# Six gate products cut in halves and put between the steps of the delta rule's inverses

## What is computed

```python
def first_block(x, ...):
    for l in range(DEPTH):                                  # two layers
        h = rmsnorm(x, norm_mix_g[l])
        proj = h @ w_in[l]
        (qa, ka, va, qd, kd, vd, beta_logit, decay_logit, z, gate_logit) = jnp.split(proj, offsets, axis=-1)
        ...
        y_attn = grid_attention(qa, ka, va) @ w_o_attn[l]
        qkv = jax.nn.silu(centred_depthwise_conv(jnp.concatenate([qd, kd, vd], axis=-1), dn_conv_w[l]))
        ...
        o = bidir_gated_deltanet(qd, kd, vd, beta, g)       # chunks of 64 tokens, 8 heads, both directions
        o = rmsnorm(o, dn_out_norm_g[l]) * jax.nn.silu(z)
        y_dn = o.reshape(b, s, DN_V) @ w_o_dn[l]
        gates = jax.nn.sigmoid(gate_logit).reshape(b, s, N_BRANCH, D_MODEL)
        mixed = gates[:, :, 0] * y_attn + gates[:, :, 1] * y_dn
        x = x + mixed @ w_out[l]
        ...                                                 # a feed-forward part
def second_block(x, mem, ...):
    for l in range(DEPTH):                                  # two layers
        h = _rmsnorm(x, norm_g[l])
        z = h @ w_in[l]
        ...
```

## Time and profile before

| | us |
|---|---|
| median of 3 runs | 3692.01 (3689.04 to 3694.11) |
| the profiled execution | 3687.55 |
| its span, first to last instruction | 3685.6 |
| TensorE busy in the span | 3377.2 |
| VectorE busy | 1894.9 |
| ScalarE busy | 1555.4 |
| GpSimd busy | 218.6 |

### The profile page before, as it was taken

One profiled execution on the slowest core, in us unless ns is written; L12 is line 12 of the kernel. 1 busy time (PEld: TensorE's weight loads), 2 busy tenths in 40 slices (PEclk: granted clock), 3 DMA queues, 4 the chain that ended last, 5 costly groups with the idle time before them and its releaser, 6 DMA issues. The chain is left out here.

```text
span 3685.6 us, 61547 instructions
## 1 busy us (share of the span) xinstructions
PE 3377.2 (92%) x26780; PEld 2658.0 (72%) x26780; DVE 1894.9 (51%) x2834; ACT 1555.4 (42%) x2612; POOL 218.6 (6%) x204
## 2 busy tenths in 40 slices
PE   7887899999998887999999988989999979989999
PEld 4576777778875676877788865767777757767787
DVE  5565554575566555554756554452434544534343
ACT  6533223433347433233433355546443455463432
POOL 0032330000000131300000000000000000000000
PEclk9897999999999988999999999999999989999999
DMA  3000003332231000023233231211122312111222
GB/s 136 29 14 19 25 14 124 102 97 92 92 116 46 13 19 25 23 75 101 87 97 103 84 114 52 76 38 60 55 83 71 114 32 78 52 55 61 66 69 94
DMA packets 74925, 249.09 MB, mean 68 GB/s; under 512 B 9249, under 2 KB 10913, under 8 KB 73377
## 3 DMA queue, kind: packets, MB, share of 16 engines
q1 hardware_dynamic: 74656, 245.16, 20.4%
HBM read 237.82 MB, written 6.29 MB: 66 GB/s over the span
## 5 line engine op out<-in xcount | busy, mean ns | idle before, releaser
L470 PE MATMUL psum<-s_h,s_w 128*128 128x512 f32 (+1 forms) x6864 | 1672.7, 400 | 50.9 <-DVE s_h L1782 20.4
L470 PEld LDWEIGHTS psum<-s_h,s_w 128*128 128x128 f32 (+1 forms) x6864 | 1294.1, 191 | 360.7 <-issue 43.3
L1782 DVE TENSOR_TENSOR s_w<-s_stage,s_w 128x1024 fp32r<-128x1024 f32 (+2 forms) x468 | 522.7, 1119 | 493.8 <-ACT s_w L1169 491.5
L1169 ACT ACTIVATE s_w<-s_stage 128x1024 fp32r<-128x1024 f32 (+2 forms) x468 | 450.9, 966 | 304.4 <-PE psum L470 279.4
L1169 ACT ACTIVATE s_tmp<-psum 128x512 f32<-128x512 f32 (+2 forms) x192 | 110.0, 573 | 364.1 <-PE psum L470 356.3
L470 PE MATMUL psum<-s_ffa,s_w 128*128 128x512 f32 x1056 | 249.0, 396 | 3.8 <-DVE s_ffa L1782 3.8
L470 PEld LDWEIGHTS psum<-s_ffa,s_w 128*128 128x128 f32 x1056 | 197.5, 187 | 54.3 <-DVE s_ffa L1782 6.4
L470 PE MATMUL psum<-s_oR,s_w 128*128 128x512 f32 (+1 forms) x960 | 223.2, 383 | 11.5 <-DVE s_w L1782 5.7
L1169 ACT ACT_TABLE_LOAD x169 | 216.8, 1283 | 7.8 <-DMA s_x<-xT 4.8
L470 PEld LDWEIGHTS psum<-s_oR,s_w 128*128 128x128 f32 x960 | 169.0, 192 | 47.9 <-DVE s_w L1782 6.7
L1169 ACT ACTIVATE s_E<-psum,s_nm 128x256 f32<-128x256 f32 (+3 forms) x224 | 114.5, 516 | 195.4 <-DVE s_nm L1864 195.4
(11 more groups left out here) (252 smaller groups left out, 3491.9 us busy)
## 6 DMA issues: line engine op xcount, KB each, us to landing
s_stage<-w SPq DMA_DIRECT2D x192, 512.0 KB, 3.3
s_stage<-wup SPq DMA_DIRECT2D x88, 512.0 KB, 3.3
s_stage<-wo SPq DMA_DIRECT2D x32, 512.0 KB, 3.3
s_stage<-wdn SPq DMA_DIRECT2D x32, 512.0 KB, 3.5
s_stage<-wdn SPq DMA_DIRECT2D x16, 384.0 KB, 3.1
spill<-s_x SPq DMA_DIRECT2D x2, 2048.0 KB, 8.3
s_stage<-woa SPq DMA_DIRECT2D x16, 256.0 KB, 2.7
s_x<-spill SPq DMA_DIRECT2D x2, 2048.0 KB, 8.1
```

The costliest lines, as they stand in the source:

```text
L470: return self.e.matmul(out, left, right, start=first, stop=last, skip_group_check=True)
L1169: return self.e.activation(out, src, func, **kw)
L1782: return self.e.tensor_tensor(out, a, b, op)
```

## The change

Six of the eight gate products of branch d leave branch d. A new generator `plug` makes them in halves of 12 matmuls. `plugged` lets it take one half at the listed turns: two at the start of the delta rule's scalars, five in `units(0)`, one in `chain(l, 0)`, four in `units(1)`. ACT takes the tanh at once into a new tile `early2`. Meanwhile the other fill products there make their weights only one product ahead instead of two.

The triangle mask on the queries' part is no longer a multiplication by POOL: DVE takes the minimum with a constant that is 0 inside the triangle and very negative outside it, so that the exponential is zero there; DVE then writes the query products straight to M2, and the 16 multiplications of POOL fall away. In the second block `normal` runs all eight columns at once behind q product 0. The size of the DMA scratch goes from 4096 to 2048.

```diff
-    def mixed(self, l, attention, scalars, begun, project, gates):
+    def mixed(self, l, attention, scalars, begun, project, gates, plug):
...
-        beside(abreast(scalars, begun, delayed(project(0, (1,)), 2)), fill, 1, 1)
-        beside(units(0), fill, 5, 6)
-        beside(self.chain(l, 0), fill, 5, 6)
+        beside(plugged(abreast(scalars, begun, delayed(project(0, (1,)), 2)), plug, (0, 1)), fill, 1, 1)
+        beside(plugged(units(0), plug, (4, 5, 21, 22, 33)), fill, 5, 6)
+        beside(plugged(self.chain(l, 0), plug, (0,)), fill, 5, 6)
...
-        beside(units(1), fill, 5, 4)
+        beside(plugged(units(1), plug, (4, 5, 21, 22)), fill, 5, 4)
...
+def plugged(steps, plug, turns):
+    for n, _ in enumerate(steps):
+        if n in turns:
+            next(plug, None)
+        yield
...
-            if name == "d" or c >= 4:
+            if c >= (PLUGS if name == "d" else 4):
...
+    def plug(self, l, hi, lo, ht):
+        for c in range(PLUGS):
+            yield from self.lin_steps((l, "d", "g", c), self.d["w1"][l, 30 + c], 8, hi, lo, ht, 4, ("act_mix", l, "d", c))
...
-                self.ahead(key)
+                self.ahead(key, 1)
...
+    def plug(self, l):
+        for c in range(PLUGS):
+            key = (l, "d", "g", c)
+            self.ahead(key, 1)
+            yield
+            g = self.k.tmp[l, "d", c, "gate"] = self.m.early2[:, c, :]
+            self.w.wait_ge(*self.prod(key))
+            self.f(g, self.bank(key), ACT.Tanh, scale=0.5).then_inc(*self.up("act_mix", l, "d", c))
+            yield
...
-        uppers = self.uppers(("two", l), hi, 4)
+        uppers = self.uppers(("two", l), hi, 8)
...
-        self.e.tensor_scalar(X, Pm, 0.0, None, ALU.min).then_inc(*self.up("vec_unit", key, "a1"))
+        self.tt(v8(X), v8(Pm), B(m.cstm[:, M_BU + r, None, :], 1, 8), ALU.min).then_inc(*self.up("vec_unit", key, "a1"))
...
-            self.tt(X[:, s], X[:, s], self.bank((both, "kq", e))[:, 256:512], ALU.mult).then_inc(*self.up("vec_unit", key, "q", e))
+            self.tt(m.M2[:, r, jp, s], X[:, s], self.bank((both, "kq", e))[:, 256:512], ALU.mult).then_inc(*self.up("vec_unit", key, "q", e))
...
-        self.w.wait_ge(*self.at("pool_unit", key, "M2"))
+        self.w.wait_ge(*self.at("vec_unit", key, "q", 1))
+        self.w.wait_ge(*self.at("pool_unit", key, "X1"))
...
-                next(normal, None)
-                next(normal, None)
+                for _ in normal:
+                    pass
...
-        self.w.wait_ge(*self.at("vec_unit", key, "q", 1))
-        self.tt(v8(m.M2[:, r, jp, :]), v8(X), over(M_TU + r), ALU.mult).then_inc(*self.up("pool_unit", key, "M2"))
```

More of the change, by code:

```diff
@@ L21 @@
 LAG = 3
+PLUGS = 6
 ORDER_A = (4, 0, 5, 1, 6, 2, 7, 3)
@@ L36 @@
 M_ID = 14
-M_N = 15
+M_BU = 15
+M_N = 17
 def constants():
@@ L60, in constants @@
     zm[:, M_ID] = row == c64
+    zm[:, M_BU] = np.where(row <= c64, 0.0, NEG)
+    zm[:, M_BU + 1] = np.where(row >= c64, 0.0, NEG)
     for k in range(6):
@@ L364, in __init__ @@
                 self.oat, self.o = sm("oat", [128, 4, T]), sm("dno", [128, 4, T])
+                self.early2 = sm("early", [128, PLUGS, T])
                 self.zs = [sm("qkv", [128, 2, 2, T]), self.x[:, 4:8, :].rearrange("p (a b) t -> p a b t", a=2)]
@@ L494, in lin, with lin_steps @@
         last.then_inc(*self.up("prod", self.used - 1))
-    def lin_steps(self, key, src, kt, hi, lo, made, per):
+    def lin_steps(self, key, src, kt, hi, lo, made, per, free=None):
         whi, wlo = self.weights(key, src, kt)
@@ L506, in lin_steps @@
                 last.then_inc(*self.up("prod", n))
+                if free is not None:
+                    self.give(key, free)
             if k % per == per - 1:
@@ L728, in layer1 @@
         self.mixed(l, lambda: self.attention(A, f), scalars, begun, lambda g, js: self.project(l, g, js, hi, lo, ht),
-                   lambda: itertools.chain(self.gates(l, hi, lo, ht), self.early(l, hi, lo, ht)))
+                   lambda: itertools.chain(self.gates(l, hi, lo, ht), self.early(l, hi, lo, ht)),
+                   self.plug(l, hi, lo, ht))
         def branch(name, c, gate, w, made, a):
-            if name == "d" or c >= 4:
+            if c >= (PLUGS if name == "d" else 4):
                 self.lin((l, name, "g", c), wt[l, gate + c], 8, hi, lo, ht)
@@ L917, in chain @@
         for r in range(2):
-            self.after([("act_unit", (l, g, 1, r), "w"), ("vec_unit", (l, g, 1, r), "w"), ("pool_unit", (l, g, 1, r), "M2")])
+            self.after([("act_unit", (l, g, 1, r), "w"), ("vec_unit", (l, g, 1, r), "w"), ("vec_unit", (l, g, 1, r), "q", 1)])
         heads = [(jp, e) for jp in range(2) for e in range(2)]
@@ L1377, in layer1 @@
         self.mixed(l, lambda: self.attention(("A", l), grid_attn(m, l)), scalars, begun, lambda g, js: self.project(l, g, js),
-                   lambda: itertools.chain(self.gates(l), self.early(l)))
+                   lambda: itertools.chain(self.gates(l), self.early(l)), self.plug(l))
         self.w.wait_ge(*self.at("vec_chain", (l, 1), "o", 7, 1))
@@ L1962, in layer1 @@
         for c in range(8):
-            self.ahead((l, "d", "g", c))
+            if c >= PLUGS:
+                self.ahead((l, "d", "g", c))
             self.ahead((l, "d", c))
@@ L2171, in gates, with plug @@
             yield
+    def plug(self, l):
+        for c in range(PLUGS):
+            self.ahead((l, "d", "g", c), 1)
+            yield
+            yield
     def early(self, l):
         for c in range(4):
-            self.ahead((l, "a", "g", c))
+            self.ahead((l, "a", "g", c), 1)
             for _ in range(5):
@@ L2691 @@
     from concourse.bass_utils import run_bass_kernel_spmd as _run
-    nc = _bacc.Bacc("TRN2", target_bir_lowering=False, num_devices=1, dynamic_dma_scratch_size=4096)
+    nc = _bacc.Bacc("TRN2", target_bir_lowering=False, num_devices=1, dynamic_dma_scratch_size=2048)
     arrays = arrange(inputs)
```

## The result

| | before | after |
|---|---|---|
| median of 4 runs, us | 3693.06 (3689.04 to 3698.52) | 3643.89 (3643.32 to 3646.85) |
| profiled execution, us | 3687.55 | 3644.41 |
| its span, us | 3685.6 | 3642.6 |

The ratio after to before is 0.9868, 95% interval 0.985 to 0.9885: the change makes the kernel 1.3% faster, 49 us by the medians. The two profiled executions differ by 43.1 us.

What follows compares the result with a forecast made beforehand. The prediction took PE as the bound, busy for 3377.2 of 3685.6 us. Its terms summed to -28.0 us for a first-block layer, -56 for two, with 0 for the second block: from 3692.0 to 3636 us, range 3612 to 3662.

Steps and rivals of the forecast that it cites:

- Branch d: Branch d of each first-block layer: six gate products of 5.48 us leave it, -32.9 us, with no loss booked.
- The pairs: Halves in the inverses' waits: `units(0)` pair 0 +1.5, pair 1 -4.0; `units(1)` pair 0 -2.0, pair 1 -1.5 us a layer.
- the mask itself: First block's triangle mask as a DVE minimum: +1 us per layer, other end +5.
- The step that failed: `units(0)` pair 1: at most 5.1 us won, -4.0 taken, as the second wait hangs on DVE's operations.
- The sign that the prediction gave for the clock: In `units`, the profile after would show the first doubling step of 128 matmuls near 3.9 us.
- The longer minimum: DVE's two-input minimum in the mask: 688 ns against 420, 0.27 us more for each direction and pair, 8 per layer.
- The chain's place: End of `units(0)` and start of the chain (turns 33 and 0): +6.8 us a layer, ends +5.5 and +9.
- Pushing: Half of turn 33: projection, convolution and zeroing of S come 2.74 us later, and the wait stays at 4.29.
- the low clock for the second half: Half of the chain's turn 0, behind the wait for S: costs 2.74 to 5.3 us.
- The start: Two halves at turns 0 and 1 of the delta rule: +2.1 us a layer, between ends 0 and +5.5.
- The weights and the tail: Weights one product ahead, and branch a's first weights behind ACT's norm work: +1 us per layer (0 to +3).
- The second block: All columns normed at once: the 10.21 us wait only moves behind q product 1's scaling; 0 (-0.4 to +2) per layer.

Runs made afterwards that it cites:

- e1: The changed kernel with the mask again a multiplication by POOL and the second block's norm again in two sets of four columns: 3653.29 us, ratio 0.990.
- e2: The kernel before with only the mask as a minimum and POOL's 16 multiplications gone: 3676.45 us, ratio 0.9959.
- e6: The changed kernel with S set to zero by DVE at pair 1's last doubling step instead of the chain's start: 3643.7 us, ratio 0.9861.
- the experiment: The changed kernel without the two halves at turns 0 and 1, one gate product going back to branch d: 3652.62 us, ratio 0.9883.
- e9: The changed kernel with the second block's input normed in two sets of four columns again: 3642.71 us, ratio 0.987.
- e3: The kernel before with only the second block's input normed in one go, all eight columns: 3700.25 us, ratio 1.0018.

## Why the prediction was right, and where it was not

3636 was forecast, 3643.89 measured, inside the range of 3612 to 3662.

**Branch d** (-32.9) came out to the tenth in both layers, and the 72 matmuls on `s_odR` run without a wait. That term carried the sign of the result, and its safety lay in a stretch that was full.

**The pairs** were forecast at -6.0 a layer together and measured at -6.4 and -7.6. The sum is near, and in part by luck, since the reasons behind it were mixed. The prediction let the halves and the shorter POOL chain share the gain and gave the mask itself +1. e1 and e2 part them: in the three places with waits on POOL the halves alone are about neutral, the mask alone is worth 10 us a layer. Without the mask and the second block's part the change gives 37 us by the ratio, 42 by the medians (e1), and not 49. The step that failed is "-4.0, since the second wait hangs on DVE's operations, which don't get shorter": DVE's operations there in turn waited for POOL (12.2 us in the earlier trace rows, 4.8 with the mask alone, 0.0 in the kernel after). The sign that the prediction gave for the clock came true in two pairs and in part in the third: the doubling step of 128 matmuls takes 3.93 and 3.95 us in the pairs of `units(1)`, but in pair 1 of `units(0)` 4.98 in layer 0 (3.95 in layer 1) where 3.9 was forecast. That is 1 us of the difference between -3.2 and -4.5.

The longer minimum takes what was booked. Groups of DVE in the kernel after, 184 to 570 us, then of the mask alone, 184 to 560:

```profile
L1812 DVE TENSOR_TENSOR s_xb<-s_cstm,s_xb 128x512 f32<-128x512 f32 x16 | 21.0, 1371 | 0.0
...
L1812 DVE TENSOR_TENSOR s_xb<-s_xb,s_cstm 128x512 f32<-128x512 f32 x8 | 5.5, 684 | 0.0
```

```profile
L1785 DVE TENSOR_TENSOR s_xb<-s_cstm,s_xb 128x512 f32<-128x512 f32 x16 | 25.1, 1616 | 4.8 <-POOL s_xb L2461 4.8
```

The minimum takes 684 ns. It has both inputs in SBUF, but stands where POOL has nothing to do (in pair 1 of `units(0)` at 272.48 and 274.41, while POOL stands still until 278.18), so the exclusion that the Trainium skill states (page "SBUF — State Buffer", section "Who interferes with whom") did not strike it. The operations beside POOL took 1644 ns before. With 16 of POOL's 128 mask operations gone and nothing else changed they still take 1616, with the halves alone 1581, and only with both 1371. So the masks that went don't by themselves give that time back to DVE; why both together do is open.

**The chain's place** was forecast as the bad one, +6.8, and it was worse: +9.6 and +8.4. Pushing (2.6 and 1.5 us measured for 2.74, the wait of 4.3 unchanged) and the low clock for the second half (4.7 us, forecast 2.74 to 5.3) were right. The rest, sized at 1 us for ACT's early tanh, came out at 2.3. The rows point to that tanh, which waits 9.60 us for the half in the chain and holds the projection's tanh behind it; no run parts it from the rest. That the zeroing of S was the cause of the wait, as the prediction took from the releaser's name, is wrong (e6).

**The start** was forecast at +2.1; the stretch shows +5.6 and +4.0, the experiment some 2.7, all traces together 3.4 and 2.3. **The weights and the tail** at +1: 1.0 and 1.1.

**The second block** at 0: the wait moved behind the scaling as worked out (9.65 us for ACT's `s_tmp`, 9.5 forecast), and e9 shows no net that its interval could tell from nothing.

**What is left** of the 6 to 8 us between forecast and result: 3.5 us at the start and 2.8 at the chain in layer 0, 1.9 and 1.6 in layer 1, and the clock, partly made good by the pairs and by the mask's +1, which no stretch shows. In the second block's layer 0 the trace after loses 4 us in work that the change doesn't touch, with the same waits. The same two rows, before and after:

```profile
2281.03 4.24 PE L470 MATMUL psum<-s_v,s_U 128*128 128x62 f32 x32
```

```profile
2234.06 6.93 PE L483 MATMUL psum<-s_v,s_U 128*128 128x62 f32 x32
```

4.24 against 6.93 us for 32 matmuls, and 3.00 against 5.40 for the product behind it, after a wait of nearly the same length (4.45 and 4.17 us): the granted clock during that product is 1.00 in the one and 0.52 in the other. Such differences are in other traces too: e3, which changes nothing in the first block, takes 1.3 us more than before in the first stretch of layer 0.

## What to carry to other kernels

- Work that is moved into a wait pays only if it stands behind everything on which the end of that wait depends. The same two halves cost 8 to 10 us ahead of the projection and at the chain's first step, and less than nothing at the waits for `s_u` later in the chain. Ask of each place: who is waiting, for what, and is what I insert ahead of that?
- Count the moved product's other instructions, too: here a 0.6 us tanh, waiting for its product at the wrong place in ACT's queue, held the projection's tanh from 349.49 to 356.45, 7 us, while the half's matmuls took 4.78.
- A releaser's name says who came last, not that nothing else comes at the same time. Follow a wait back by two steps before its end is taken for a fixed cost: POOL stood behind DVE, and two masks less of it for each pair were worth 15 us alone (e2), of 49 for the whole change.

## What the runs showed of the hardware that was not expected

The kernel before scatters by 19 us (3680.8 to 3700.1) over 19 runs, and the traces show what part of it can be: in equal code the work right behind a wait of 4.45 us ran in 4.24 us in one trace, behind one of 4.17 us in 6.93 in the other, and the product after it in 3.00 and 5.40. So what a wait costs beyond its length differed by 5.1 us between two executions. Filling a wait with work can earn this, too: `units(1)` went from a granted clock of 0.95 to 1.00.
